# Depthwise convolution of a hybrid decoder step: its last tap multiplied on POOL into its own buffer and added by DVE one strip later

## What is computed

```
def causal_conv_silu(x, buf, w, b):
    xp = jnp.concatenate([buf.astype(x.dtype), x], axis=1)
    y = xp[:, 0:T] * w[0]
    for i in range(1, CONV_W):
        y = y + xp[:, i:i + T] * w[i]
    if b is not None:
        y = y + b
    return jax.nn.silu(y), xp[:, T:]
```

## Time and profile before

| | |
|---|---|
| median of 3 runs | 3574.84 us (3569.72 to 3579.85) |
| the profiled execution | 3581.62 us, its span 3579.8 us |
| mean granted TensorE clock | 0.933 of full speed |
| busy share of the span | PE 90%, DVE 60%, POOL 40%, ACT 16% |
| span of the stage `convolve` | 1069.3 to 1179.1 us, 3.1% of the span |

### The profile page before, as it was taken

One profiled execution on the slowest core, in us unless ns is written; L12 is line 12 of the kernel. 1 busy time (PEld: TensorE's weight loads), 2 busy tenths in 40 slices (PEclk: granted clock), 3 DMA queues, 4 the chain that ended last, 5 costly groups with the idle time before them and its releaser, 6 DMA issues. The chain is left out here.

```text
span 3579.8 us, 54279 instructions
## 1 busy us (share of the span) xinstructions
PE 3222.5 (90%) x22287; PEld 2964.6 (83%) x22287; DVE 2159.8 (60%) x3252; ACT 579.9 (16%) x1104; POOL 1424.2 (40%) x852
## 2 busy tenths in 40 slices
PE   7968999998984677775997999999999999999998
PEld 6935888998763577734887999999999999999998
DVE  7125997897319655356986755555465555556554
ACT  3222222122317211124322100000000000000000
POOL 4344333485424323223333443444444444444442
PEclk9989999999985788676998999999999999999999
DMA  5322333487743000316323222323223222322232
GB/s 180 99 77 82 102 98 102 126 253 226 222 128 87 13 1 1 98 50 183 111 86 138 73 87 81 94 83 91 87 83 95 81 86 83 95 84 85 84 92 98
DMA packets 415941, 360.30 MB, mean 101 GB/s; under 512 B 26362, under 2 KB 367962, under 8 KB 414309
## 3 DMA queue, kind: packets, MB, share of 16 engines
q1 hardware_dynamic: 379664, 287.06, 27.5%
q0 software_dynamic: 13440, 42.02, 3.7%
q10 hardware_dynamic: 22592, 27.59, 2.3%
HBM read 311.63 MB, written 46.20 MB: 100 GB/s over the span
## 5 line engine op out<-in xcount | busy, mean ns | idle before, releaser
L3117 POOL TENSOR_TENSOR om_ring<-om_raw,om_mask 128x1024 fp32r<-128x1024 f32 x262 | 675.7, 2579 | 906.5 <-DVE om_ring L3236 906.5
L3158 PE MATMUL om_ps<-om_h,om_ring 128*128 128x272 f32 x6144 | 779.4, 290 | 21.4 <-issue 17.8
L3158 PEld LDWEIGHTS om_ps<-om_h,om_ring 128*128 128x128 f32 x6144 | 777.0, 190 | 23.6 <-issue 23.5
L3158 PE MATMUL om_ps<-om_hid,om_ring 128*128 128x272 f32 x6144 | 770.6, 288 | 0.0
L3158 PEld LDWEIGHTS om_ps<-om_hid,om_ring 128*128 128x128 f32 x6144 | 769.8, 188 | 0.0
L3236 DVE CAST om_ring<-om_mask 128x1024 fp32r<-128x1024 f32 x262 | 453.9, 1732 | 9.1
L338 POOL TENSOR_TENSOR w_ring<-w_raw,w_mask 128x1024 fp32r<-128x1024 f32 (+2 forms) x110 | 259.5, 2379 | 344.0 <-DVE w_mask L469 192.7
L389 PE MATMUL pm_ps<-h,w_ring 128*128 128x280 f32 x2688 | 361.6, 296 | 18.1 <-issue 10.9
L389 PEld LDWEIGHTS pm_ps<-h,w_ring 128*128 128x128 f32 x2688 | 354.1, 192 | 25.9 <-issue 18.8
L3244 DVE TENSOR_TENSOR om_x<-om_x,om_ps 128x272 f32<-128x272 f32 x288 | 112.6, 432 | 359.6 <-PE om_ps L3158 354.9
L3374 ACT ACTIVATE om_relu<-om_relu 128x272 f32<-128x272 f32 x128 | 50.0, 432 | 1417.6 <-DVE om_relu L3265 1417.5
(11 more groups left out here) (526 smaller groups left out, 3808.5 us busy)
## 6 DMA issues: line engine op xcount, KB each, us to landing
om_raw<-in_w_up SPq DMA_DIRECT2D x128, 512.0 KB, 4.1
om_raw<-in_w_down SPq DMA_DIRECT2D x128, 512.0 KB, 3.6
w_raw<-in_w_in SPq DMA_DIRECT2D x112, 512.0 KB, 3.8
ao_raw<-in_w_out SPq DMA_DIRECT2D x32, 384.0 KB, 3.9
as_qb<-q_rows SPq DMA_DIRECT2D x32, 256.0 KB
projT<-pm_stage ACTq DMA_DIRECT2D x56, 140.0 KB
conv_x<-projT SPq DMA_DIRECT2D x28, 280.0 KB, 2.8
xT_scratch<-ln_xT SPq DMA_DIRECT2D x1, 4480.0 KB, 15.5
```

The costliest lines, as they stand in the source:

```text
L3117: pool.tensor_tensor(f32r(ring[:, s, 1, half_of(q)]), raw[:, q, :], mask[:, q, :], ALU.subtract).then_inc(split[q], 1)
L3158: ins = pe.matmul(ps[bank][:, 0:HM], w, f32r(src[:, b, k, kept_half(half)]), start=first, stop=last)
```

## The change

The third of DVE's three taps is taken off DVE. POOL, after its four copies of strip f, multiplies the strip by the fourth weight into a new buffer `tap` (two slots), once the convolution of strip f - 2 is done. DVE does two taps of strip f, and after them one tensor_tensor that adds `tap` of strip f - 1 to `y` of strip f - 1; that signals `conv`. `conv_y` has three buffers. ACT's SiLU of strip f comes in iteration f + 2, the copy of its transpose out of PSUM in iteration f + 3, the squares begin one iteration later, and the streams of ACT and DVE run one iteration longer.

```diff
-AT_GATES, AT_SQUARES = 4, 24
+AT_GATES, AT_SQUARES = 4, 25
...
-        y = sbuf("conv_y", [P, 2, YW])
+        y, tap = sbuf("conv_y", [P, 3, YW]), sbuf("conv_tap", [P, 2, YW])
...
+        two_taps, last_tap = sem("conv_two_taps"), sem("conv_last_tap")
...
@@ POOL, behind the four copies of strip f
+                pool.wait_ge(laid, f + 1)
+                if f >= 2:
+                    pool.wait_ge(conv, f - 1)
+                pool.tensor_scalar(tap[:, f % 2, :], xp[:, f % R, 3:3 + YW], par[:, f, 3:4], None, ALU.mult
+                                   ).then_inc(last_tap, 1)
...
@@ ACT
-            for f in range(NCONV + 2):
+            for f in range(NCONV + 3):
                 if f < NCONV:
                     act.wait_ge(laid, f + 1)
-                    if f >= 2:
-                        act.wait_ge(act_ready, f - 1)
-                    act.activation(y[:, f % 2, :], xp[:, f % R, 0:YW], ACT.Identity, bias=par[:, f, 4:5],
+                    if f >= 3:
+                        act.wait_ge(act_ready, f - 2)
+                    act.activation(y[:, f % 3, :], xp[:, f % R, 0:YW], ACT.Identity, bias=par[:, f, 4:5],
                                    scale=par[:, f, 0:1]).then_inc(first, 1)
-                if 1 <= f <= NCONV:
-                    silu(f - 1)
-                if f >= 2 and f - 2 in nth:
-                    tokens_out(f - 2)
+                if 2 <= f <= NCONV + 1:
+                    silu(f - 2)
+                if f >= 3 and f - 3 in nth:
+                    tokens_out(f - 3)
...
@@ DVE
-            for f in range(NCONV + 2):
+            for f in range(NCONV + 3):
                 if f < NCONV:
                     dve.wait_ge(first, f + 1)
-                    for i in range(1, 4):
+                    for i in range(1, 3):
...
-                        if i < 3:
+                        if i < 2:
                             step(ins)
-                    ins.then_inc(conv, 1)
+                    ins.then_inc(two_taps, 1)
+                if 1 <= f <= NCONV:
+                    dve.wait_ge(two_taps, f)
+                    dve.wait_ge(last_tap, f)
+                    dve.tensor_tensor(y[:, (f - 1) % 3, :], y[:, (f - 1) % 3, :], tap[:, (f - 1) % 2, :], ALU.add
+                                      ).then_inc(conv, 1)
```

More of the change, by code:

```diff
@@ L633, in silu @@
                 act.wait_ge(conv, f + 1)
-                act.activation(dest(f)[:, 0:TP], y[:, f % 2, 0:TP], ACT.Silu)
-                own = y[:, f % 2, RAW:RAW + DB * 7 - 3]
+                act.activation(dest(f)[:, 0:TP], y[:, f % 3, 0:TP], ACT.Silu)
+                own = y[:, f % 3, RAW:RAW + DB * 7 - 3]
                 src = AP(tensor=own.tensor, offset=own.offset, ap=[list(own.ap[0]), [7, DB], [1, DT]])
@@ L745, in _ @@
             dve.wait_ge(par_in, 32)
-            for f in range(NCONV + 2):
+            for f in range(NCONV + 3):
                 if f < NCONV:
                     dve.wait_ge(first, f + 1)
-                    for i in range(1, 4):
-                        ins = dve.scalar_tensor_tensor(out=y[:, f % 2, :], in0=xp[:, f % R, i:i + YW],
-                                                       scalar=par[:, f, i:i + 1], in1=y[:, f % 2, :],
+                    for i in range(1, 3):
+                        ins = dve.scalar_tensor_tensor(out=y[:, f % 3, :], in0=xp[:, f % R, i:i + YW],
+                                                       scalar=par[:, f, i:i + 1], in1=y[:, f % 3, :],
                                                        op0=ALU.mult, op1=ALU.add)
-                        if i < 3:
+                        if i < 2:
                             step(ins)
-                    ins.then_inc(conv, 1)
+                    ins.then_inc(two_taps, 1)
[4 more added lines that the diff above has]
+                                      ).then_inc(conv, 1)
                 if f >= 4 and f % 4 == 0:
```

## The result

| | before | after |
|---|---|---|
| median | 3574.84 us (7 runs, 3569.72 to 3579.85) | 3588.47 us (7 runs, 3586.72 to 3591.59) |
| ratio, 95% interval | | 1.0038 [1.0025, 1.005] |
| span of the profiled execution | 3579.8 us | 3585.0 us |
| stage `convolve` (POOL's first MEMSET to DVE's first instruction of the next stage) | 110.0 us | 126.2 us |
| first tap of strip 0 to that of strip 25 | 77.5 us | 93.7 us |

The account below looks back on a forecast made before the run. The prediction took DVE to bound the steady stretch of `convolve`. It added 12.4 us before strip 25 and -0.6 in the tail, +12 on the median of 3574.8, for 3587 us (chance 0.55), range 3572 to 3600.

Parts of the forecast that it names:

- the prediction's own signs of being wrong: In the changed profile: taps staying at 860 ns, POOL's multiplication over 1.1 us, or another stage moving.
- the ring: Steady strips: `conv` of strip f - 2, multiplication f, copies f + 1, ACT's first tap, DVE's taps, addition closing the loop.
- if it misses, behind the addition: POOL's fourth copy of strip f + 1: done at 2.63 us, or at 3.19 if held until DVE's addition.
- DVE's saving: DVE, each strip: third tap becomes an addition of 0.79 us, so 2.38 us instead of 2.57, 0.19 saved.
- POOL's multiplication: POOL's new instruction on 616 columns: taken as 0.75 us, between bounds of 0.61 and 1.22.
- The exclusion: POOL's multiplication and DVE's two-input instructions shut each other out, lengthening DVE's second tap by 0.44 us a strip.
- An iteration: One steady strip after the change: 3.20 us, 0.63 more than before.
- The count: The 25 iterations before strip 25: one at 0, fifteen 9.5, four 1.6, five 1.3 us, together 12.4 more.
- The tail: From strip 25 to the stage's end: 26.2 us instead of 26.8, so -0.6.
- DVE alone counts: Rival, chance 0.17: copies slip in and POOL's order delays nobody; a strip costs 2.82 us, +5, 3580 us.
- A slow multiplication: Rival, chance 0.18: POOL's multiplication takes 1.22 us, a normal iteration 3.6 to 3.7; +22, 3597 us.
- No exclusion, the other side: Rival, chance 0.10: POOL's multiplication does not hold up DVE's taps, so the saving stays; -6, 3569 us.

Follow-up runs that it names:

- run 4: Changed kernel with POOL writing zeros into the tap buffer instead of multiplying, last tap left out: 3.06 us a strip, stage 113.7 us.
- run 5: Changed kernel without POOL's two copies into `conv_last3`, which is zeroed once instead: 3.37 us a strip, stage 119.9 us.
- run 9: Kernel of run 8 with five buffers for the strips instead of four: 2.50 us a strip, stage 104.1 us.
- run 6: Changed kernel with POOL's copies of strip f + 1 ahead of the multiplication of strip f: 3.52 us a strip, stage 121.4 us.
- run 7: Kernel of run 6 also without POOL's two copies into `conv_last3`: 3.20 us a strip, stage 115.3 us.
- run 2: Changed kernel with POOL's multiplication as tensor_tensor, the weight as second input: 3.62 us a strip, stage 128.4 us.
- run 8: Kernel of run 6 with POOL writing zeros instead of multiplying, last tap left out: 2.89 us a strip, stage 110.2 us.
- run 1: Changed kernel with all three taps on DVE again, no POOL multiplication, rest of the change kept: 3566.56 us, ratio 0.9979 to the kernel before, stage 106.8 us.

## Why the prediction was right, and where it was not

The forecast was 3587, slower, by +12; measured 3588.5, +13.6. The frame is the one named: POOL's copies come late, ACT's first tap waits for them and DVE for ACT (44.4 us where it was 28.7). But the nearness is partly luck. The stage grew by 16.2, above the 12 of the sum, and the program's median by less than the stage. And two of the prediction's own signs of being wrong are there: the taps stay at 860 ns (median 860, mean 875) and the multiplication takes over 1.1 us (1.82). It named two causes, a ring that begins with the multiplication's wait for `conv` and DVE's taps held up by the multiplication. Neither binds the steady strip of the changed kernel; the ring does in runs 4 and 5. What binds is the exclusion in the other direction: one of POOL's copies is held up until DVE's addition has ended, and ACT's first tap starts behind it. The prediction had this as a side case ("if it misses, behind the addition"). Step by step:

- **DVE's saving.** Forecast 0.19 us a strip, 2.38 instead of 2.57. Right: additions of 0.80 (0.79 forecast), and 2.41 a strip in run 9.
- **POOL's multiplication.** This term failed. "I take 0.75", between 0.61 and 1.22; it is 1.82, beyond both bounds. The upper bound was an addition with two inputs, taken as dearer than a multiplication with one. On POOL it is the other way round: 1.21 us for tensor_tensor, 1.75 with a number and 1.82 with a weight. The Trainium skill ("GPSIMD Engine Reference", section 3.1) puts bodies of one or two operations at 1.03 cycles a column; 1.82 us for 616 columns is 3.0 ns a column, some 3.5 of the 1.2 GHz cycles it names, so the trace does not agree for this instruction.
- **The exclusion.** Forecast 0.44 us a strip; the taps grew by 17 ns, 1 us over the stage. Two things were wrong. In the steady strip, DVE's tap comes 0.87 us after the multiplication has begun (1158.25, 1159.12), since ACT's tap lies between. And the multiplication doesn't hold DVE up for its whole length. In the changed kernel this pair met (POOL, then DVE):

```profile
1101.40 2.49 POOL L629 TENSOR_SCALAR conv_tap<-conv_x,conv_par 128x616 f32<-128x616 f32 x1 [1.58 <-DVE conv_y L765]
```

```profile
1102.24 1.25 DVE L756 SCALAR_TENSOR_TENSOR conv_y<-conv_x,conv_par,conv_y 128x616 f32<-128x616 f32 x1
```

  POOL waited 0.67 us, so it began at about 1102.07 and ended at 1103.89. The tap ended at 1103.49, before it. With the 0.72 us that the prediction gives an instruction that was held up, it was let go at 1102.77. It was held for 0.70 of the 1.82 us. Worked out in the same way, 26 held-up taps of the changed kernel and runs 5, 6 and 7 all give 0.69 or 0.70. Rows 6 and 7 had shown an addition that ended 0.81 after POOL's, and I took that for every instruction.
- **An iteration.** Forecast 3.20, measured 3.63. With 1.82 in place of 0.75 the ring alone gives (0.05 + 1.82 + 1.8 + 0.98 + 2.47) / 2 = 3.56, and POOL's own time 1.82 + 1.8 = 3.6. Both sums come near, but they hold 1.8 us of copies that are mostly waits for DVE; runs 2 and 6 show that neither binds, since 0.6 us less of multiplication or the opened ring leaves 3.62 and 3.52. The path that closes in all of them is ACT's first tap, two taps, addition, the copy held up by the addition. With four copies of 0.62 together, as where none is held up, the ring's sum would be 2.97: an estimate, since no run shows it.
- **The count.** Between strips 0 and 25 the forecast was 0 + 9.5 + 1.6 + 1.3 = 12.4; measured, period by period against the kernel before, it is 0.4 + 13.6 + 1.3 + 0.9 = 16.2. So the ordinary fifteen were mis-sized, ten of them at 1.06 to 1.09 each where 0.63 was taken, and the others were nearly right.
- **The tail.** Forecast -0.6; from the first tap of strip 25 to the end it took 26.5 before and 26.4 after. Right in sign, 0.1 in size.
- **"The transfer isn't late."** True at 3.63 us a strip. Runs 8 and 9 show it late at 2.9: this loop was in the change too, behind the others.
- **"ACT's third buffer removes no wait seen in the rows."** Wrong in its effect: with the later SiLU it frees DVE of 2.2 us of waits (run 1), which the multiplication hid.
- **The rivals.** *DVE alone counts* needed copies that slip in; in every steady strip two of the four are held up. *A slow multiplication* is nearly run 2: with 1.21 us a strip takes 3.62, as it said (3.6 to 3.7), and the stage 18.4 us more where it said 22. The changed kernel's 1.82 us, 0.6 slower still, cost no more. *No exclusion, the other side* is ruled out by run 4, where POOL's write holds up no tap: 113.7 us, over the 110.0 of before.

What stays open: why POOL's tensor_scalar takes 3 ns a column when it holds up DVE for 0.7 us only, how the 3.20 of run 7 divides between the exclusion and hand-overs, and what the changed kernel would take if none of its copies were held up.

## What to carry to other kernels

Before work goes from a bound engine to another, count what the bound engine really loses: here a tap of 0.86 became an addition of 0.79, and POOL was given 1.82 for it. Where a helper engine stands in a ring (copies, first tap, taps, addition), its order decides as much as its load: an instruction ahead of copies that others wait for delays them all, and here it pushed them under the other engine's long instructions, where a copy of 0.2 us takes 0.8. Each wait that goes shows the next one (3.63, 3.5, 2.9, 2.5). The easier gains of this stage lay in a single buffer of its tail and in ACT's slack, worth 9.7 us of it together. The first could be read from the rows of before; the second was found by a trial of the order without its main part.

## What the runs showed of the chip

- POOL, 128x616 f32: write 0.61 us, tensor_tensor 1.21, tensor_scalar by a number 1.75, by a weight of each partition 1.82.
- tensor_scalar on POOL holds up DVE's instructions with two SBUF inputs for 0.70 us of its 1.82. The tensor_tensor of run 2 does so for 1.14 of its 1.21 us: it still lengthened a tap that began 0.89 us after it, by 0.12 us (two taps 1.88 instead of 1.76).
- A POOL copy of 0.2 us beside DVE's taps and additions takes 0.75 to 0.80 us: it ends with the DVE instruction that runs. So four copies took 1.8 us in the changed kernel and 2.4 in run 2.
- POOL's write holds up no tap for more than 0.06 us (the longest 918 ns in run 4). The Trainium skill ("SBUF — State Buffer", "Who interferes with whom") has DVE's second input contend only with POOL instructions that read; the trace agrees on that, and disagrees on a lock for the whole instruction (0.70 of 1.82 us).
